# Down product with tokens as the stationary side and 512 weight columns streamed, left-over tokens on VectorE

## What is computed

```
cap = CAPACITY_FACTOR * T // N_EXPERTS
g, idx = lax.top_k(jnp.swapaxes(aff, 1, 2), cap)
hid = jax.nn.silu(jnp.einsum('becd,edf->becf', xs, w_gate)) * \
    jnp.einsum('becd,edf->becf', xs, w_up)
ys = jnp.einsum('becf,efd->becd', hid, w_down) * g[..., None].astype(u.dtype)
```

## Time and profile before

| | us |
|---|---|
| median of 3 runs | 2525.51 |
| lowest, highest | 2521.96, 2526.09 |
| profiled execution, its time | 2524.75 |
| its span, first to last instruction | 2522.9 |
| phases 1 and 2, to the first gate matmul | 233.9 |
| one expert in the loop of 15 | 141.94 |

### The profile page before, as it was taken

The page is one execution under the profiler, slowest core; times in us unless marked ns, Lnnn a source line. Parts: engine busy times, 40 slices in busy tenths (PEclk is TensorE's granted clock), DMA queues, the critical chain, the costliest instruction groups (busy, mean ns, idle before and its releaser), DMA issues.

```text
span 2522.9 us, 54344 instructions
## 1 busy us (share of the span) xinstructions
PE 2432.7 (96%) x20310; PEld 2423.2 (96%) x20310; DVE 1317.0 (52%) x1751; ACT 1212.2 (48%) x1798; POOL 686.6 (27%) x858
## 2 busy tenths in 40 slices
PE   7974999999999999999999999999999999999997
PEld 7973999999999999999999999999999999999997
DVE  5646545555454545555454545555454545555475
ACT  5653444444444444444444444444444444444464
POOL 0011406042332406042322405042332405042101
PEclk9976999999999999999999999999999999999998
DMA  7651566666656666666656666666656666666794
GB/s 219 197 163 52 182 200 192 197 186 208 183 183 201 182 200 190 198 186 209 183 183 200 182 200 190 197 186 209 183 183 200 183 200 189 198 186 209 221 321 176
DMA packets 437005, 486.02 MB, mean 193 GB/s; under 512 B 22241, under 2 KB 417233, under 8 KB 436978
## 3 DMA queue, kind: packets, MB, share of 16 engines
q1 hardware_dynamic: 411250, 433.81, 55.1%
q0 software_dynamic: 21120, 35.08, 6.1%
q10 hardware_dynamic: 4608, 16.78, 1.7%
HBM read 443.26 MB, written 42.50 MB: 193 GB/s over the span
## 4 chain that ended last, share of the span: by engine, by line
PE 96%; DVE 2%; DMA 1%; ACT 0%; issue 0%; POOL 0%; SPq 0%; DVEq 0%; ACTq 0%; POOLq 0%
PE bank L1232 93%; PE bank L1237 3%; DVE marks_v L1011 0%; DMA nmix<-in_norm_mix 0%; DMA x_left<-u_rows,idx_chunk 0%; ACT u_t L724 0%; DVE picks L1095 0%; DVE pooled_lo L919 0%; DVE pw L946 0%; DVE key_t L1035 0%; DVE y_rows L1224 0%; ACT junk L847 0%; ACT squares L694 0%; ACT pooled_hi L707 0%; DVE flag L1018 0%
## 5 line engine op out<-in xcount | busy, mean ns | idle before, releaser
L1129 DVE TENSOR_TENSOR w_lo<-raw,w_hi 128x1024 fp32r<-128x1024 f32 x765 | 936.3, 1224 | 550.3 <-ACT w_hi L785 509.0
L1232 PE MATMUL bank<-x_hi,w_hi 128*128 128x258 f32 x4096 | 1160.2, 283 | 5.2 <-issue 3.3
L1232 PE MATMUL bank<-x_lo,w_hi 128*128 128x258 f32 x4096 | 1162.8, 284 | 0.0
L1232 PE MATMUL bank<-x_hi,w_lo 128*128 128x258 f32 x4096 | 1145.4, 280 | 0.0
L785 ACT ACTIVATE w_hi<-raw 128x1024 fp32r<-128x1024 f32 x765 | 804.9, 1052 | 238.5 <-PE bank L1232 202.4
L1232 PEld LDWEIGHTS bank<-x_hi,w_hi 128*128 128x128 f32 x4096 | 777.3, 190 | 9.8 <-issue 9.7
L1232 PEld LDWEIGHTS bank<-x_hi,w_lo 128*128 128x128 f32 x4096 | 781.9, 191 | 0.0
L1232 PEld LDWEIGHTS bank<-x_lo,w_hi 128*128 128x128 f32 x4096 | 776.7, 190 | 0.0
L1232 PE MATMUL bank<-hid_hi,w_hi 128*128 128x258 f32 x2048 | 584.0, 285 | 0.0
L1232 PE MATMUL bank<-hid_lo,w_hi 128*128 128x258 f32 x2048 | 580.9, 284 | 0.0
L1232 PE MATMUL bank<-hid_hi,w_lo 128*128 128x258 f32 x2048 | 573.9, 280 | 0.0
(11 more groups left out here) (168 smaller groups left out, 1191.1 us busy)
## 6 DMA issues: line engine op xcount, KB each, us to landing
raw<-in_moe_w_gate SPq DMA_DIRECT2D x128, 1024.0 KB
raw<-in_moe_w_up SPq DMA_DIRECT2D x128, 1024.0 KB
raw<-in_moe_w_down SPq DMA_DIRECT2D x128, 1024.0 KB
h_in<-in_x SPq DMA_DIRECT2D x18, 512.0 KB, 5.7
x_rows<-h_acc ACTq DMA_DIRECT2D x16, 512.0 KB, 5.6
out<-x_rows ACTq DMA_DIRECT2D x16, 512.0 KB, 4.5
h_acc<-h_mid SPq DMA_DIRECT2D x17, 448.0 KB, 5.0
u_rows<-u_out SPq DMA_DIRECT2D x17, 448.0 KB, 3.0
```

What stands on the lines that cost most here:

```text
L1129: nc.vector.tensor_tensor(w_lo[:, a % 4], quarter_view(a // 2 % 4, a % 2), w_hi[:, a % 4].bitcast(f32), ALU.subtract).then_inc(split_lo, 1)
L1232: return nc.tensor.matmul(dst, lhs, rhs, start=start, stop=stop)
```

## The change

- Down product of experts 0 to 14: the hidden tokens are the stationary side (128 tokens), and 512 columns of w_down rows are streamed. `down_row(n, k)` handles 128 hidden channels: 2 token blocks x 3 terms x 2 halves of the width = 12 matmuls into banks 4 to 7, accumulated over k = 0 to 15. The result stands as token rows, so the transposes of y and the copies `y_t` go; `rows_out` on ScalarE multiplies by the gate straight from PSUM at the start of the next expert's first gate quarter.
- The two left-over tokens: `add_left(n, k)` on VectorE, acc_left (128 x 2 x 1024) += raw row x hidden value of the token (a scalar of each partition), 32 instructions of 128x1024 an expert. Rows 0 and 1 stand in gate block 3, rows 2 to 13 in the down stage, rows 14 and 15 in the first gate block of the next expert. `fold_left` sums over the partitions with a matrix of ones in fp32 behind that block (four matmuls to 32 rows each); ScalarE copies, GpSimd packs four rows by a DMA, multiplies by the gate and adds them to `h_halves` by an indirect DMA.
- Residuals w_lo: 36 of an expert on VectorE, the last 12 (down rows 4 to 15) on GpSimd (`split_lo_p`), in its queue behind the gather. The last add of an odd row on VectorE also waits for GpSimd's residual of that row.
- Six raw buffers instead of four; the loads that replace down rows wait for left_done. Down pieces are two rows of 1024 channels, contiguous.
- The sends of the next list wait for quarters 10 to 28 instead of 2 to 20.
- Router in phase 1: `rw_wide` (128x32, 16 columns used) is the stationary side, u_t is streamed (128 columns), four groups of 32 PSUM rows; VectorE copies the partial sums, and one matmul with `fold` sums the groups.
- The last expert keeps the old form (`last_down_quarter`).

The core of the diff:

```diff
-        raw = sb("raw", [P, 4, 8 * 256], f32)
+        raw = sb("raw", [P, SLOTS, 8 * 256], f32)
...
+        def split_view(idx, down=False):
+
+            if down:
+                return raw[:, idx // 2 % SLOTS, idx % 2 * D:(idx % 2 + 1) * D].rearrange("p (k f) -> p k f", k=8)
+            return quarter_view(idx // 2 % SLOTS, idx % 2)
...
+                for m in range(SLOTS, 24):
+                    if m - SLOTS < 16:
+                        sp.wait_ge(split_lo, DVE_SPLITS * n + 2 * (m - SLOTS) + 2)
+                    else:
+                        sp.wait_ge(left_done, 32 * n + 4 * (m - SLOTS - 16) + 4)
+                    if m < 16:
+                        gate_up_piece(n, m)
+                    else:
+                        down_rows(n, m)
+                for m in range(SLOTS):
+                    i = m + 24 - SLOTS - 16
+                    sp.wait_ge(left_done, 32 * n + 4 * i + 4)
+                    gate_up_piece(n + 1, m)
...
-                    pool.wait_ge(quarters, QE * n + c + 2)
+                    pool.wait_ge(quarters, QE * n + c + 10)
...
-                pool.wait_ge(y_rows_done, 5 * n + 5)
+                for a in range(DVE_SPLITS, 48):
+                    pool.wait_ge(split_hi, QE * n + a + 1)
+                    nc.gpsimd.tensor_tensor(w_lo[:, a % 4], split_view(a, True), w_hi[:, a % 4].bitcast(f32),
+                                            ALU.subtract).then_inc(split_lo_p, 1)
+                pool.wait_ge(y_rows_done, 4 * n + 4)
...
+                pool.wait_ge(quad_done, n + 1)
+                pool.wait_ge(carrier_set, CARRIES * n + 4 + NT)
+                carry_wait()
+                pool.dma_start(y_four[:], y_quad[0:P:QUAD, :]).then_inc(quad_packed, 16)
+                pool.wait_ge(quad_packed, 16 * n + 16)
+                nc.gpsimd.tensor_tensor(y_small[:], y_four[:],
+                                        gates_now[0:2 * LEFT, 2:3].broadcast_to([2 * LEFT, 512]),
+                                        ALU.mult).then_inc(small_done, 1)
+                pool.wait_ge(small_done, n + 1)
+                pool.wait_ge(carrier_set, CARRIES * n + 5 + NT)
+                carry_wait()
+                pool.indirect_dma_start(h_halves, bass.IndirectOffsetOnAxis(ap=idx_small[0:2 * LEFT, :], axis=0),
                                         y_small[:], None, compute_op=ALU.add).then_inc(scattered, 16)
...
+            def rows_out(n):
+
+                act.wait_ge(scattered, 48 * n)
+                act.wait_ge(list_kept, 3 * n + 3)
+                act.wait_ge(quarters, QE * n + QE)
+                for f in range(4):
+                    b_, half = f // 2, f % 2
+                    nc.scalar.activation(y_rows[:, b_, half * 512:half * 512 + 512], bank[:, 4 + f, :], ACT.Copy,
+                                         scale=gates_now[:, b_:b_ + 1]).then_inc(y_rows_done, 1)
...
+            def down(n):
+                for k in range(KF):
+                    split_ahead(n, 32 + k + 3, True)
+                    if 8 <= k < 8 + XT:
+                        round_x(k - 8, XT * n + XT + k - 7)
...
+                    dve.wait_ge(part_routed, upto(i0, j, -3))
+                    if upto(i0, 0, -5) > 0:
+                        dve.wait_ge(routed, upto(i0, j, -5))
+                    nc.vector.tensor_copy(partial[:, s, :], bank[:, 7, s * P:(s + 1) * P]).then_inc(part_out, 1)
...
+            def wait_rows_split(n, k):
+
+                if 32 + k < DVE_SPLITS:
+                    dve.wait_ge(split_lo, DVE_SPLITS * n + 32 + k + 1)
+                else:
+                    dve.wait_ge(split_lo_p, (48 - DVE_SPLITS) * n + 32 + k + 1 - DVE_SPLITS)
+
+            def add_left(n, k):
+
+                piece = 16 + k // 2
+                rows = raw[:, piece % SLOTS, k % 2 * D:(k % 2 + 1) * D]
+                dve.wait_ge(loaded_w[piece % SLOTS], loads_of(n, piece))
+                dve.wait_ge(hid_left_done, KF * n + k + 1)
+                if k == 0:
+                    dve.wait_ge(folded, n)
+                for t in range(LEFT):
+                    by = hid_left[:, k, t:t + 1]
+                    if k == 0:
+                        nc.vector.tensor_scalar(acc_left[:, t], rows, by, None, ALU.mult).then_inc(left_done, 1)
+                    else:
+                        dve.wait_ge(left_done, 32 * n + 2 * k + t - 1)
+                        if k % 2 == 1 and t == LEFT - 1:
+                            wait_rows_split(n, k)
+                        nc.vector.scalar_tensor_tensor(out=acc_left[:, t], in0=rows, scalar=by, in1=acc_left[:, t],
+                                                       op0=ALU.mult, op1=ALU.add).then_inc(left_done, 1)
...
+                for k in range(KF):
+                    if k < KF - 4:
+                        add_left(n, k + 2)
+                    if 8 <= k < 8 + XT:
+                        rest_of_x(k - 8, XT * n + XT + k - 7)
+                    if k + 3 >= KF:
+                        split_rest(n, 32 + k + 3)
+                gate_up(n + 1, 0, left_of=n)
...
-                        last = mm(bank[:, 6, ds(NE * (i0 - 3) + (BODY * NE) * j, NE)], u_t[:, k * P:(k + 1) * P],
-                                  rw[:, k, :], k == 0, k == KD - 1)
-                    last.then_inc(routed, 1)
+                        quad = slice(QUAD * (k % 4), QUAD * (k % 4) + QUAD)
+                        last = mm(bank[quad, 7, s * P:(s + 1) * P], rw_wide[:, k, :], u_t[:, k * P:(k + 1) * P],
+                                  k < 4, k >= 4)
+                    last.then_inc(part_routed, 1)
...
+                    pe.wait_ge(part_out, upto(i0, j, -3))
+                    mm(bank[:, 6, ds(NE * (i0 - 3) + (BODY * NE) * j, NE)], partial[:, (i0 - 3) % 2, :],
+                       const("fold"), True, True).then_inc(routed, 1)
...
+            def down_row(n, k):
+
+                if k + 32 < DVE_SPLITS:
+                    pe.wait_ge(split_lo, DVE_SPLITS * n + 32 + k + 1)
+                else:
+                    pe.wait_ge(split_lo_p, (48 - DVE_SPLITS) * n + 32 + k + 1 - DVE_SPLITS)
+                if k == 0:
+                    pe.wait_ge(hid_lo_done, KF * n + KF - 4)
+                    pe.wait_ge(y_rows_done, 4 * n)
+                    pe.wait_ge(quad_done, n)
+                if k == 4:
+                    pe.wait_ge(hid_lo_done, KF * n + KF)
+                s = k % 4
+                for b in range(2):
+                    toks = slice(b * P, b * P + P)
+                    terms = ((hid_hi, w_hi), (hid_hi, w_lo), (hid_lo, w_hi))
+                    for i, (h, w) in enumerate(terms):
+                        for half in range(2):
+                            last = mm(bank[:, 4 + 2 * b + half, :], h[:, k, toks],
+                                      w[:, s, 4 * half:4 * half + 4].rearrange("p m j -> p (m j)"),
+                                      k == 0 and i == 0, k == KF - 1 and i == 2)
+                last.then_inc(quarters, 1)
+
+            def fold_left(n):
+
+                pe.wait_ge(left_done, 32 * n + 32)
+                pe.wait_ge(y_rows_done, 4 * n + 4)
+                for half in range(2):
+                    for t in range(LEFT):
+                        j = half * LEFT + t
+                        last = mm(bank[j * QUAD:(j + 1) * QUAD, 4, :], ones[:, 0:QUAD],
+                                  acc_left[:, t, half * 512:half * 512 + 512], True, True)
+                last.then_inc(folded, 1)
...
+                for k in range(KF):
+                    down_row(n, k)
...
-                for f in range(4):
-                    turn_y(n, f % 2, f // 2, 4 + f)
-                pe.wait_ge(y_rows_done, 5 * n + 1)
-
-                pe.wait_ge(y_left_done, n + 1)
-                turn_block(bank[0:SMALL_ROWS, 4, 0:P], y_left[:].rearrange("p m t -> p (m t)"))\
-                    .then_inc(y_turned, 1)
-
-            with pe.Fori(0, 4) as b:
+                gate_up(n + 1, 0)
+                fold_left(n)
```

More of the change, by code:

```diff
@@ L119, in constants @@
     put("tok_lo", tok % 16)
+    put("fold", (k % QUAD)[:, None] == np.arange(NE)[None, :])
     put("tok", tok)
@@ L317, in encoder_kernel @@
         stored_u = [sem(f"stored_u{s}") for s in range(2)]
-        loaded_w = [sem(f"loaded_w{s}") for s in range(4)]
+        loaded_w = [sem(f"loaded_w{s}") for s in range(SLOTS)]
         weights_scaled = sem("weights_scaled")
@@ L387, in encoder_kernel @@
         y_turned = sem("y_turned")
-        y_left_done = sem("y_left_done")
+        hid_left_done = sem("hid_left_done")
+        left_done = sem("left_done")
+        folded = sem("folded")
+        quad_done = sem("quad_done")
+        quad_packed = sem("quad_packed")
+        small_done = sem("small_done")
         y_rows_done = sem("y_rows_done")
@@ L527, in _ @@
+            for m in range(SLOTS, 24):
+                sp.wait_ge(split_lo, DVE_SPLITS * (NE - 1) + 2 * (m - SLOTS) + 2)
+                if m < 16:
+                    gate_up_piece(NE - 1, m)
+                else:
```

(57 more changed lines are left out.)

233 lines of the change are left out of this document (128 added, 105 removed).

## The result

The changed kernel takes 2796.11 us (median of 4 runs, 2794.26 to 2798.01) against 2525.60 (4 runs, 2521.96 to 2526.09): 1.1075 times as long, interval 1.1055 to 1.1094. The profiled execution took 2794.26 us, its span is 2792.4. The forecast was 2810, its range of eight in ten 2560 to 2930.

A forecast was written before the change was run, and what follows sets the result against it. PE bounds the kernel (96% busy); after the change, VectorE and GpSimd excluding each other bounds the down stage. Expert 91.9 + 67 + 2.2 = 161.1 against 141.94, 15 times +287, router -2: 2810 us, eight in ten 2560 to 2930.

The forecast's parts named there:

- The exclusion: Down stage: two-input VectorE multiply-adds (1.19 us) and GpSimd splits (2.32 us) exclude each other for their whole length.
- The stage: Down stage of an expert: 67 us (61 to 74), PE idling about 15 to 20, mostly at row 11.
- half clock: Down stage: after idling, PE's granted clock falls to 0.50, costing 2.2 us an expert (0 to 4).
- PE waits for neither: Down stage: GpSimd's splits stand behind its gather (three issues, about 1 us each) and hold back the scatter, without delaying PE.
- Matmuls of 512 columns: Down stage: 192 matmuls of 0.2255 us (0.2133 to 0.2375), 43.3 us in all (41.0 to 45.6).
- rival (c): Down stage: 512-column matmuls cost per column as before, giving away 2.3 us an expert, invisible where PE waits; no chance given.
- The fold: Next expert's first gate block: summing left-over tokens over partitions costs PE 2.2 us (0.9 to 3.6).
- The router: Phase 1: +0.2 to -1.3 us a tile, cut short at about -0.6; -10 to +4 over 19 tiles, -2 taken.
- gate quarters: Gate and up of an expert: 768 matmuls take 91.9 us, with no PE idle between quarters.
- Rival (a): Down stage: no exclusion that matters, the new work hides under PE, stage 45.2 us, total 2483 us; chance 0.16.

The follow-up runs named there:

- e1: Changed kernel with VectorE's multiply-adds given one tensor input instead of two, GpSimd's splits kept, left-over tokens come out wrong: 2504.75 us, ratio 0.9921.
- e5: Changed kernel with all 48 w_lo splits on VectorE and the left-over multiply-adds spread over gate block 3, down stage and next first gate block: 2499.98 us, ratio 0.9911.
- e7: e5 with ScalarE's wait for the last scatter, its loads and the final norm's steps two quarters later in the last expert: 2495.69 us, ratio 0.9889.
- e4: Kernel before the change with only the new router of phase 1: 2510.76 us, ratio 0.9944.

## Why the prediction was right

**The exclusion: right.** The step rested on tensor_tensor rows only the earlier trace rows and took the multiply-add to be the same. After and e1 together show that it is: 3.35 us for a pair, against 1.19 + 2.32 + 0.1 = 3.61 in the sum. The turns overlap a little, so the size was high by 0.26 a pair, 2.6 us for ten. One count behind it was off, without harm: 97 is the number of carriers longer than 0.26 us; 108 begin inside a VectorE split, all 108 end 0.045 to 0.059 us after it, and the 222 others take 0.22 at most.

**The stage: 67 forecast, 67.25 measured**, but partly by terms that cancel. VectorE came 5.5 us into the stage, not 3.2, because the multiply-adds of row 1 and two splits stand ahead of its list copies; the pairs were cheaper; x_lo was there at 681.29, 51.3 us in, against 51.4. PE idled 15.6 us (15 to 20 forecast, and my sum implied 19.8), its matmuls took 1.5 more (0.2335 against 0.2255), and half clock 4.5 rather than 2.2, since there were two idle stretches, not one.

**"PE waits for neither", of the gather's three issues: wrong.** GpSimd's first split stands behind the carrier, which took 1.08 us, and two issues of 1.90 and 2.00 that I had counted at about 1: it began 12.4 us into the stage, and PE waited 3.72 at row 4. In e1 it began at 10.0 and PE waited 1.14; so 2.6 of the 3.7 is the collision (the carrier and the issues held up by it included), and 1.1 is queue order that I should have counted.

**Matmuls of 512 columns: inside the bounds, near the upper one.** 0.2335 us against 0.2375 for cost per column as before, and 0.2255 taken. My reason, that 16 and 128 columns cost the same, told of short fp32 matmuls and not of this. By the Trainium skill's figure (0.2158 us, an estimate from "TensorE: Matmul & The Clock Gate", Back-to-back issue gap) the 192 matmuls would take 3.4 us less; the trace doesn't have that. This comes near rival (c), and as I said it doesn't show where PE waits; in e5 and e7, where PE is the bound, it costs 15 x 1.5 = 23 us against the 0.2255 taken.

**The fold: 2.2 forecast, 0.99 measured**, the lower bound: four groups run side by side.

**The router: -2 forecast, out of its range of -10 to +4.** Phases 1 and 2 shrank by 15.5 us, and by itself the router is worth 13.3 (e4). A tile gained 0.61 us, just the "about -0.6" I had worked out; 19 x 0.6 = 11.4 was in my own text, and I then took -2 without a row for it. What else is in the 15.5 was not followed. The 38 fold matmuls of 16 columns take 7.2 us of busy time for all tiles and did not cancel it.

**The last expert: not in the sum at all.** I had looked at who waits for the scatter inside the loop and missed the one instruction behind the loop that does: ScalarE's load for the final norm, at +11.5 us.

**The total.** 2810 - 18.2 (fold) + 3.7 (stage) + 0.9 (gate quarters 91.96) - 13.5 (phases 1 and 2) + 11.5 (last expert) = 2794.4, against 2794.26. What made the loss, the stage's growth from 50.1 us to 67, 15 x 17, was right to 2%, by the cancelling named above. The misses outside it were 10 to 18 us each and of both signs; that the total is off by 14 us of 2810 and not by more is luck in that part.

**Rival (a)**, which e1 brings about, was priced at 2483 and came at 2504.75. By the spans: phases 1 and 2 -12 against its sum, the loop +23 (stage 48.05 rather than 45.2, +43; the fold -18; small pieces -2), the last expert +11. So even without the exclusion the change, with its splits where they were, was worth only 20 us, 14 of them from phases 1 and 2.

## What to carry to other kernels

Before work moves to two idle engines, count the inputs that each instruction reads from SBUF: VectorE with two of them beside a GpSimd instruction that reads SBUF was one engine here, not two, and the busy times came near to adding up (3.35 us a pair, of 1.19 and 2.32 alone). The best repair of those tried was to put all of it on VectorE, spread over the stages where that engine has slack, and not to halve it. And follow a result that is now made later to its last reader in the whole program, behind the loop too.

## What the runs showed of the hardware that was not expected

Matmuls into separate groups of 32 PSUM rows run side by side also in fp32: of the eight records of the fold, of 512 columns each, four begin between 560.14 and 560.16 us and four between 560.59 and 560.61, and all take 0.99 us, as long as four of 0.2335 would take one by one. 16 router matmuls of 128 columns take 0.64 us, again with starts in fours. Going back to full width costs a tenth of a microsecond at most that the trace shows (the matmul behind the fold begins at 561.13, the next one 0.23 later rather than 0.12); before, the first matmul behind the 16 router matmuls of full width had the same (0.20 to the next), so the width is not shown to be the reason.

An indirect DMA issued by GpSimd takes longer when it begins inside a two-input VectorE instruction, though not each of them does. Groups of the gather, after; in e1, above, the first is 1001 ns:

```profile
L611 POOL DMA_INDIRECT x_rows<-u_rows,idx x32 | 60.6, 1895 | 46.3 <-DVE gates L1199 39.1 <-issue 7.2
L614 POOL DMA_INDIRECT x_left<-u_rows,idx_chunk x16 | 13.8, 864 | 4.9 <-issue 4.9
```

e1 differs from it only in the second input of the multiply-add, and e5 has 1863 with no GpSimd split at all. So the issue itself is held up, by about 0.9 us each. The second line is the exception: this third issue begins within 0.03 us of the start of a multiply-add, runs beside it to its own end, and takes 0.86 in all 15 experts; in e5, at a split that begins as close to it, it takes 1.94. In the kernel before, where the split begins 0.07 to 0.09 us after the second issue, that issue takes 0.96, and in the two experts in which the split began 0.6 us before it, 1.45. So an issue that begins well inside such an instruction was held each time, one that begins before it was not, and what decides when both begin together is open.
